# Stage ends and feed-forward openings of a two-block transformer kernel: another order of row-vector product, inverse and weight differences

## The chip, the cores and the metric

One core of one Trainium2 chip runs one program. The metric is the device time of a whole launch in microseconds. The median of 3 runs of the kernel before is 2208.19 us, lowest 2207.74, highest 2209.24.

## The reference

256 tokens of 1,024 values pass two blocks in fp32. The first block joins a recurrent branch and 16-head attention, followed by a retrieval layer of 16,384 experts. The second block has four feed-forward stages with a convolution stage and an attention stage between them. Each stage end and each feed-forward stage is this (cut):

```python
def rms_norm(x, g):
    x32 = x.astype(jnp.float32)
    y = x32 * lax.rsqrt(jnp.mean(x32 * x32, axis=-1, keepdims=True) + RMS_EPS)
    return (y * g.astype(jnp.float32)).astype(x.dtype)

def swiglu_ffn(h, w_gate_up, w_down):
    gate, up = jnp.split(h @ w_gate_up, 2, axis=-1)
    return (jax.nn.silu(gate) * up) @ w_down
...
        f = swiglu_ffn(rms_norm(x, ffn_norm_pre[layer, 0]), ffn_w_gate_up[layer, 0], ffn_w_down[layer, 0])
        x = x + MACARON_WEIGHT * rms_norm(f, ffn_norm_post[layer, 0])
```

The convolution and the attention stage end with `x = x + rms_norm(y, mix_norm_post[layer])` in the same way.

## The kernel before

**Weights.** All weights come as one stream of 664 chunks of 128 x 1024 fp32 (512 KB), in the order in which they are used, through a ring of RING = 3 buffers `raw`. ACT copies a chunk to fp32r (`whi`, L442, or L447 inside loops) and DVE subtracts to get what the copy lost (`wlo`, L915, or L920 inside loops). This is `split(c)` on both engines: ACT's part waits until the chunk has landed and until chunk c - 3 has been used by PE (`used`), DVE's part waits for ACT's. PE multiplies three times for each tile: high by high, high by low, low by high (L1586 to L1588 where the activations move, L1965 to L1967 where rows of tokens come out). SP loads chunk c + 3 when `wlo` of chunk c is made.

**Stage ends.** `bound(B)`, B = 0 to 7, stands in the program of each engine. B = 0 and 1 end the two halves of the first block; B = 2, 4, 5 and 7 end the feed-forward stages ffn0 to ffn3; B = 3 ends the convolution stage (`cout`), B = 6 the attention stage (`qo`). The stage's result lies in PSUM as four pieces of 128 tokens x 512 values (`wide`, r = 2t + half). ACT squares each piece and sums it (L482), and takes a root for each t (L487); DVE prepares one operand of the root (`half_of`, L960), inverts (`invert`, L965), and makes the new rows piece by piece in the order (t, half) = (0,0), (1,0), (0,1), (1,1): for B from 2 on `scaled` (L975) multiplies a piece by the inverse and by the norm vector (`rows_of`), and `added` (L981) adds it to the residual `htok` (tile res). Meanwhile PE runs 60 small bf16 matmuls without use (L1649). When the first two pieces are new, PE transposes them (`turn_half(B, 0)`, L1658), ACT scales and rounds the transposed tiles to `XH` (L497), DVE makes their rest `XL` (`lo_of_turned`, L945), and PE begins the next stage with its first two chunks (`first_pair`): the high products of tiles 0 to 3 (L1613, L1614), then `turn_half(B, 1)`, then the low products of tiles 0 to 3 (L1621), then high and low of tiles 4 to 7. `first_pair` waits at its head for `wlo` of both chunks.

**Feed-forward.** With b the stage's first chunk, chunks b and b + 1 are gate and up of the first 128 hidden values, then come gate, up, down in turn for the next ones: b + 2 gate, b + 3 up, b + 4 down of the first, b + 5 gate, b + 6 up and so on. The factor of the norm ahead of a stage is found while the first products run: ACT takes its root (`in_root`, L512), DVE inverts it (`in_inverse`, L1011), PE spreads it over the partitions (`in_spread`, L1640), and DVE copies it to `rstd` (`in_rstd`, L1015). DVE multiplies the gate by it (`gate_scaled`, L1430), ACT applies SiLU (L785), DVE forms the hidden values (`h_full`, L1436 and L1439), ACT rounds them (`h_hi`, L791) and DVE takes the rest (L1441), on which the down chunk waits. ACT has to load a table before its first SiLU (`preload`, L471). The order of the work on each engine is that in which the code issues it, and an engine that waits holds everything behind it.

## Time and profile before

| | |
|---|---|
| median of 3 runs | 2208.19 us |
| the profiled execution | 2207.9 us |
| its span on the core | 2205.9 us |
| PE busy | 2129.3 us, 97% |
| DVE busy | 1534.0 us, 70% |
| ACT busy | 1176.9 us, 53% |
| mean granted clock of PE | 0.991 |

The profiled execution is 0.3 us under the median, and 2.0 us of it lie outside the span. PE's busy time is made of modelled ends, each matmul's overlapping the next, so short pauses hardly show in it: they are read from the distance between starts. The lengths below are read in the same way, from one start to the next, wherever an order of work is followed.

### The profile page before, as it was taken

The numbers are of one execution on the slowest core, as the hardware profiler recorded it, in microseconds if no ns is written. First come the engines' busy times: TensorE is split into PE (matmuls) and PEld (weight loads), VectorE is DVE, ScalarE is ACT, GpSimd is POOL, SyncE is SP. The second block draws the span as 40 slices with busy tenths as digits, with TensorE's granted clock in tenths as the row PEclk, the third lists the DMA queues.
The fourth block names the chain that finished last, engine by engine and source line by source line (L and its number), as shares of the span: only waits on it lengthen the run. The fifth ranks groups of instructions, "written<-read, shape, count | busy, mean of one in ns | idle before, by whom it ended". The sixth has DMA issues, their size and how long they took to land.

```text
span 2205.9 us, 42158 instructions
## 1 busy us (share of the span) xinstructions
PE 2129.3 (97%) x15056; PEld 1953.2 (89%) x15056; DVE 1534.0 (70%) x2584; ACT 1176.9 (53%) x1996; POOL 52.8 (2%) x77
## 2 busy tenths in 40 slices
PE   7989999999999999999999999989999999999998
PEld 7888889999999988888888999878999999988997
DVE  7577665999899985555556666866666666676665
ACT  4755445656567664455455445445445444655444
POOL 0020000000100000000003000000000000000000
PEclk9999999999999999999999999999999999999999
DMA  5442354545443345555555665314554555444554
GB/s 204 153 146 94 106 174 152 186 170 183 159 138 119 131 155 196 192 191 194 195 191 193 231 218 192 134 46 165 184 186 154 183 186 184 168 146 137 185 185 142
DMA packets 101117, 366.47 MB, mean 166 GB/s; under 512 B 11504, under 2 KB 12144, under 8 KB 100528
## 3 DMA queue, kind: packets, MB, share of 16 engines
q1 hardware_dynamic: 97776, 352.59, 46.8%
q0 software_dynamic: 3264, 12.85, 1.6%
q8 instruction: 49, 0.80, 0.1%
q14 instruction: 28, 0.23, 0.0%
HBM read 363.29 MB, written 2.10 MB: 166 GB/s over the span
## 4 chain that ended last, share of the span: by engine, by line
PE 78%; DVE 12%; issue 5%; ACT 4%; DVEq 1%; DMA 0%; ACTq 0%
PE acc L1586 14%; PE acc L1588 13%; PE acc L1587 13%; PE wide L1965 9%; PE wide L1966 9%; PE wide L1967 9%; DVE wlo L915 3%; DVE arena L1372 2%; DVE res L1358 2%; ACT whi L442 1%; PE acc L2037 1%; PE sums L1797 1%; PE wide L1705 1%; PE wide L1707 1%; PE wide L1706 1%
## 5 line engine op out<-in xcount | busy, mean ns | idle before, releaser
L1586 PE MATMUL acc<-XH,whi 128*128 128x256 f32 (+1 forms) x3104 | 891.3, 287 | 9.9 <-DVE wlo L915 6.7
L1587 PE MATMUL acc<-XL,whi 128*128 128x256 f32 (+1 forms) x3104 | 878.6, 283 | 0.0
L1588 PE MATMUL acc<-XH,wlo 128*128 128x256 f32 (+1 forms) x3104 | 878.5, 283 | 0.0
L920 DVE TENSOR_TENSOR wlo<-raw,whi 128x1024 fp32r<-128x1024 f32 x396 | 484.6, 1225 | 304.5 <-ACT whi L447 284.5
L1586 PEld LDWEIGHTS acc<-XH,whi 128*128 128x128 f32 x3104 | 594.7, 192 | 23.7 <-DVE wlo L915 11.3
L1587 PEld LDWEIGHTS acc<-XL,whi 128*128 128x128 f32 x3104 | 595.0, 192 | 3.3
L1588 PEld LDWEIGHTS acc<-XH,wlo 128*128 128x128 f32 x3104 | 594.7, 192 | 0.0
L447 ACT ACTIVATE whi<-raw 128x1024 fp32r<-128x1024 f32 x456 | 479.8, 1053 | 182.8 <-PE wide L1967 181.7
L915 DVE TENSOR_TENSOR wlo<-raw,whi 128x1024 fp32r<-128x1024 f32 x268 | 328.3, 1227 | 142.1 <-ACT whi L442 131.4
L1965 PE MATMUL wide<-whi,small 128*128 128x512 f32 x896 | 351.7, 393 | 6.7 <-DVE wlo L915 3.8
L1966 PE MATMUL wide<-whi,small 128*128 128x512 f32 x896 | 350.6, 391 | 0.0
L1967 PE MATMUL wide<-wlo,small 128*128 128x512 f32 x896 | 349.6, 390 | 0.0
L442 ACT ACTIVATE whi<-raw 128x1024 fp32r<-128x1024 f32 x208 | 217.8, 1052 | 80.6 <-PE acc L1588 28.2
L1965 PEld LDWEIGHTS wide<-whi,small 128*128 128x128 f32 x896 | 169.2, 189 | 40.6 <-DVE wlo L915 4.6
L1967 PEld LDWEIGHTS wide<-wlo,small 128*128 128x128 f32 x896 | 168.8, 188 | 35.8
L1966 PEld LDWEIGHTS wide<-whi,small 128*128 128x128 f32 x896 | 169.1, 189 | 31.8
L785 ACT ACTIVATE arena<-arena 128x256 f32<-128x256 f32 x88 | 36.8, 418 | 192.5 <-DVE arena L1430 192.5
L791 ACT ACTIVATE small<-arena 128x256 fp32r<-128x256 f32 x88 | 36.7, 418 | 179.1 <-DVE arena L1439 179.1
L735 ACT ACTIVATE last_parts<-res,r2T 128x128 bf16<-128x128 bf16 x256 | 81.7, 390 | 58.3 <-DVE res L1358 58.3
L710 ACT ACTIVATE arena<-acc 128x256 f32 (+1 forms) x79 | 30.4, 385 | 94.8 <-PE acc L1588 94.6
L1441 DVE TENSOR_TENSOR small<-arena,small 128x256 fp32r<-128x256 f32 x88 | 37.4, 425 | 42.5 <-ACT small L791 42.5
L1430 DVE TENSOR_TENSOR arena<-acc,rstd 128x256 f32<-128x256 f32 x88 | 37.3, 424 | 39.3 <-PE acc L1588 38.9
(289 smaller groups left out, 2093.9 us busy)
## 6 DMA issues: line engine op xcount, KB each, us to landing
raw<-stream SPq DMA_DIRECT2D x664, 512.0 KB, 3.2
arena<-taps_in POOLq DMA_DIRECT2D x20, 256.0 KB, 4.0
arena<-rows_in POOLq DMA_DIRECT2D x7, 512.0 KB, 4.8
arena<-h_in SPq DMA_DIRECT2D x2, 544.0 KB, 4.2
res<-rgw SPq DMA_DIRECT2D x1, 1024.0 KB, 8.6
res<-tokens_in POOLq DMA_DIRECT2D x1, 1024.0 KB, 5.3
park<-res POOLq DMA_DIRECT2D x1, 1024.0 KB, 4.2
res<-park POOLq DMA_DIRECT2D x1, 1024.0 KB, 5.5
```

Source lines behind the costliest of these rows:

```text
L442: act.activation(whi[:, c % RING, :], raw[:, c % RING, :], ACT.Copy).then_inc(hi_done, 1)
L447: act.activation(whi[:, c % RING, :], raw[:, c % RING, :], ACT.Copy).then_inc(hi_done, 1)
L735: ins = act.activation(last_part(m % 2)[:, a, :], of_group(onehots, m % 2, 0)[:, a, 0, :], ACT.Copy, scale=r2T[:, bass.ds(4 * g + a, 1)])
L915: V.tensor_tensor(wlo[:, c % RING, :], raw[:, c % RING, :], whi[:, c % RING, :].bitcast(F32), ALU.subtract).then_inc(lo_done, 1)
L920: V.tensor_tensor(wlo[:, c % RING, :], raw[:, c % RING, :], whi[:, c % RING, :].bitcast(F32), ALU.subtract).then_inc(lo_done, 1)
L1358: V.tensor_tensor(pairs(onehots[:, s, 0, :]), of_tokens(e12, g), pairs(iotab[:, :]).to_broadcast([P, 8, NK // 2, 2]), ALU.is_equal)\
L1586: mm(out_, whi[:, s, w], xh, start=first, stop=False, **kw)
L1587: mm(out_, whi[:, s, w], xl, start=False, stop=False, **kw)
L1588: return mm(out_, wlo[:, s, w], xh, start=False, stop=last, **kw)
L1965: mm(dst, xh[:, x], whi[:, c % RING, w], start=first, stop=False, skip_group_check=True)
L1966: mm(dst, xl[:, x], whi[:, c % RING, w], start=False, stop=False, skip_group_check=True)
L1967: ins = mm(dst, xh[:, x], wlo[:, c % RING, w], start=False, stop=last, skip_group_check=True)
```

## The change

At stage ends from B = 2 on, the piece is multiplied by the norm vector first (`with_row`, into one of now four buffers `z`), which needs no inverse, and then one instruction multiplies by the inverse and adds the residual (`new_rows`). The weight difference (`wlo`) of the next stage's second chunk goes from before the stage end to behind the first two new pieces. In the stages that follow B = 1, 3, 4 and 6, the difference of chunk b + 2 goes between the two halves of `lo_of_turned`. 46 small matmuls instead of 60. In the opening of the feed-forward stages `in_spread` stands ahead of chunk b + 2, no longer in its middle; ACT splits b + 3 ahead of the table load, and b + 4 ahead of `h_hi`; DVE scales the first gate ahead of the difference of b + 3, and makes that of b + 4 ahead of the rest of the hidden values. The DVE wait on the norm vector's load comes first in the stage end.

```diff
-        z = ar(XN, 512, 2)
+        z = ar(XN, 512, 4)
...
-                in_root((1, 3, 4, 6)[f], ACT.Silu)
+                in_root((1, 3, 4, 6)[f], None)
                 split(b + 3)
+                preload(ACT.Silu)
                 silu(0, mb + 1)
+                split(b + 4)
                 h_hi(0, mb + 1, None)
...
-                    split_loop(c + 2, i, 6) if i is not None else split(c + 2)
+                    if k > 0:
+                        split_loop(c + 2, i, 6) if i is not None else split(c + 2)
...
+                def with_row(r):
+                    t, half = PIECES[r]
+                    dve.wait_ge(sem("out_sq"), 4 * B + r + 1)
+                    V.tensor_tensor(z[:, r, :], wide[:, r, :], rows_of[B - 1][:, half * 512:half * 512 + 512],
+                                    ALU.mult).then_inc(sem("with_row"), 1)
...
+                        dve.wait_ge(sem("with_row"), 4 * (B - 2) + NEW_ORDER.index((t, half)) + 1)
+                        ins = V.scalar_tensor_tensor(out=piece(htok, t, half), in0=z[:, r, :], scalar=inv,
+                                                     in1=piece(htok, t, half), op0=ALU.mult, op1=ALU.add)
...
                 else:
                     half_of(0)
-                if B > 0:
-                    dve.wait_ge(sem(f"row{B - 1}"), 16)
-                invert(0)
-                scaled(0, 0, 0)
-                half_of(1)
-                added(0, 0, 0)
-                invert(1)
-                for n in range(1, 4):
-                    scaled(*NEW_ORDER[n], n)
-                    added(*NEW_ORDER[n], n)
+                    with_row(0)
+                    invert(0)
+                    new_rows(0, 0)
+                    half_of(1)
+                    with_row(2)
+                    invert(1)
+                    new_rows(1, 0)
+                    split(BASE[ENDS[B]] + COUNT[ENDS[B]] + 1)
+                    with_row(1)
+                    new_rows(0, 1)
+                    with_row(3)
+                    new_rows(1, 1)
                 if NEXT[B] is not None:
-                    lo_of_turned(SPLIT[NEXT[B]], gain_of(NEXT[B]), turned_into)
+                    lo_of_turned(SPLIT[NEXT[B]], gain_of(NEXT[B]), turned_into, range(4))
+                    if B in (1, 3, 4, 6):
+                        split(BASE[ENDS[B]] + COUNT[ENDS[B]] + AHEAD)
+                    lo_of_turned(SPLIT[NEXT[B]], gain_of(NEXT[B]), turned_into, range(4, DT))
...
-                split(b + 2)
                 in_inverse((1, 3, 4, 6)[f])
-                split(b + 3)
                 in_rstd((1, 3, 4, 6)[f])
                 gate_scaled(0, b % RING, b + 1)
-                h_full(0, (b + 1) % RING, b + 2, mb + 1)
+                split(b + 3)
+                h_full(0, (b + 1) % RING, b + 2, mb + 1, b + 4)
...
-                split(b + 3 * MT - 1 + 2)
                 bound((2, 4, 5, 7)[f])
...
-                for _ in range((96, 84, 60, 60, 60, 60, 60)[B]):
+                for _ in range((96, 84, 46, 46, 46, 46, 46)[B]):
...
-                    gate(c, c + j, mb + k + 1 + jm if k else None,
-                         (lambda: in_spread((1, 3, 4, 6)[f])) if k == 0 else None)
+                    if k == 0:
+                        in_spread((1, 3, 4, 6)[f])
+                    gate(c, c + j, mb + k + 1 + jm if k else None)
```

The order of instructions shows the places. DVE at the end of ffn1 (B = 4), before: the first row is the difference of the next stage's second chunk, L960 is `half_of`, L965 `invert`, L975 `scaled`, L981 `added`.

```order
L915 TENSOR_TENSOR wlo<-raw,whi 128x1024
L960 TENSOR_SCALAR tiny<-tiny 128x1
L965 RECIPROCAL tiny<-tiny 128x1
L975 SCALAR_TENSOR_TENSOR arena<-wide,tiny,arena 128x512
L960 TENSOR_SCALAR tiny<-tiny 128x1
L981 TENSOR_TENSOR res<-res,arena 128x512
L965 RECIPROCAL tiny<-tiny 128x1
L975 SCALAR_TENSOR_TENSOR arena<-wide,tiny,arena 128x512
L981 TENSOR_TENSOR res<-res,arena 128x512
L975 SCALAR_TENSOR_TENSOR arena<-wide,tiny,arena 128x512
L981 TENSOR_TENSOR res<-res,arena 128x512
L975 SCALAR_TENSOR_TENSOR arena<-wide,tiny,arena 128x512
```

The same place of the change, where L973 is `with_row`, L985 `new_rows`, L963 `half_of`, L968 `invert` and L918 the weight difference:

```order
L963 TENSOR_SCALAR tiny<-tiny 128x1
L973 TENSOR_TENSOR arena<-wide,arena 128x512
L968 RECIPROCAL tiny<-tiny 128x1
L985 SCALAR_TENSOR_TENSOR res<-arena,tiny,res 128x512
L963 TENSOR_SCALAR tiny<-tiny 128x1
L973 TENSOR_TENSOR arena<-wide,arena 128x512
L968 RECIPROCAL tiny<-tiny 128x1
L985 SCALAR_TENSOR_TENSOR res<-arena,tiny,res 128x512
L918 TENSOR_TENSOR wlo<-raw,whi 128x1024
L973 TENSOR_TENSOR arena<-wide,arena 128x512
L985 SCALAR_TENSOR_TENSOR res<-arena,tiny,res 128x512
L973 TENSOR_TENSOR arena<-wide,arena 128x512
```

The weight difference went from the first row to the ninth, behind the second new piece, and one long instruction (L973) stands ahead of the first inverse.

ACT at the opening of ffn2, before, from `in_root` (L512) on: L442 are the copies of chunks b + 3, b + 4, b + 5, b + 6, L785 SiLU, L791 `h_hi`.

```order
L512 ACTIVATE tiny<-tiny 128x2
L471 ACT_TABLE_LOAD
L471 ACTIVATE tiny<-tiny 128x1
L442 ACTIVATE whi<-raw 128x1024
L785 ACTIVATE arena<-arena 128x256
L791 ACTIVATE small<-arena 128x256
L442 ACTIVATE whi<-raw 128x1024
L785 ACTIVATE arena<-arena 128x256
L442 ACTIVATE whi<-raw 128x1024
L791 ACTIVATE small<-arena 128x256
L442 ACTIVATE whi<-raw 128x1024
```

And in the change:

```order
L512 ACTIVATE tiny<-tiny 128x2
L442 ACTIVATE whi<-raw 128x1024
L471 ACT_TABLE_LOAD
L471 ACTIVATE tiny<-tiny 128x1
L785 ACTIVATE arena<-arena 128x256
L442 ACTIVATE whi<-raw 128x1024
L791 ACTIVATE small<-arena 128x256
L785 ACTIVATE arena<-arena 128x256
L442 ACTIVATE whi<-raw 128x1024
L791 ACTIVATE small<-arena 128x256
L442 ACTIVATE whi<-raw 128x1024
```

The copy of b + 3 went ahead of the table load, and that of b + 4 ahead of the first L791.

PE in the middle of chunk b + 2 of ffn2, before:

```order
L1586 MATMUL acc<-XH,whi 128x256
L1587 MATMUL acc<-XL,whi 128x256
L1588 MATMUL acc<-XH,wlo 128x256
L1640 MATMUL sums<-ident,tiny 128x128 x2
L1586 MATMUL acc<-XH,whi 128x256
```

And in the change, between `first_pair` and chunk b + 2 (its L1641 is L1621 of before, its L1606 to L1608 are L1586 to L1588, its L1660 is L1640):

```order
L1634 MATMUL acc<-XH,wlo 128x256
L1641 MATMUL acc<-XL,whi 128x256 x8
L1660 MATMUL sums<-ident,tiny 128x128 x2
L1606 MATMUL acc<-XH,whi 128x256
L1607 MATMUL acc<-XL,whi 128x256
```

The two `in_spread` halves (L1640 before, L1660 now) went from the middle of chunk b + 2 to its front.

## Rows read from the trace of the kernel before

**Rows 1.** The page, part 1: busy time of each engine, with its share.

```profile
PE 2129.3 (97%) x15056; PEld 1953.2 (89%) x15056; DVE 1534.0 (70%) x2584; ACT 1176.9 (53%) x1996; POOL 52.8 (2%) x77
```

**Rows 2.** The waits of PE: engine, tile, line, releaser; total us, times, longest.

```profile
PE wide L1965 <- DVE wlo L915: 3.8, 4, 1.1
```

**Rows 3.** Timeline of PE, end of ffn1 and opening of ffn2: start, us, line.

```profile
1690.97 3.52 PE L1649 MATMUL sums<-iotab 128*128 128x128 bf16 x60
...
1694.69 1.09 PE L1658 MATMUL wide<-ident,res 128*128 128x128 f32 x8 [0.20 <-DVE res L981]
...
1696.01 0.36 PE L1613 MATMUL acc<-XH,whi 128*128 128x256 f32 x1 [0.22 <-ACT XH L497]
...
1697.99 1.04 PE L1658 MATMUL wide<-ident,res 128*128 128x128 f32 x8
...
1698.79 1.19 PE L1621 MATMUL acc<-XL,whi 128*128 128x256 f32 x8
...
1699.81 0.28 PE L1613 MATMUL acc<-XH,whi 128*128 128x256 f32 x1
...
1701.73 1.12 PE L1621 MATMUL acc<-XL,whi 128*128 128x256 f32 x8
...
1702.80 0.39 PE L1586 MATMUL acc<-XH,whi 128*128 128x256 f32 x1
...
1704.33 0.60 PE L1640 MATMUL sums<-ident,tiny 128*128 128x128 f32 x4
...
1704.69 0.36 PE L1586 MATMUL acc<-XH,whi 128*128 128x256 f32 x1
...
1713.68 0.38 PE L1586 MATMUL acc<-XH,whi 128*128 128x256 f32 x1
...
1717.11 0.38 PE L1586 MATMUL acc<-XH,whi 128*128 128x256 f32 x1 [0.31 <-DVE wlo L915]
```

**Rows 4.** Timeline of PE, opening of ffn0.

```profile
1176.65 0.38 PE L1586 MATMUL acc<-XH,whi 128*128 128x256 f32 x1 [0.80 <-DVE wlo L915]
```

**Rows 5.** Timeline of DVE, the same stage end as Rows 3.

```profile
1689.60 1.23 DVE L915 TENSOR_TENSOR wlo<-raw,whi 128x1024 fp32r<-128x1024 f32 x1 [0.17 <-ACT whi L442]
...
1691.38 0.16 DVE L965 RECIPROCAL tiny<-tiny 128x1 f32<-128x1 f32 x1 [0.49 <-ACT tiny L487]
...
1691.58 0.75 DVE L975 SCALAR_TENSOR_TENSOR arena<-wide,tiny,arena 128x512 f32<-128x512 f32 x1
...
1693.16 0.75 DVE L975 SCALAR_TENSOR_TENSOR arena<-wide,tiny,arena 128x512 f32<-128x512 f32 x1
...
1693.95 0.69 DVE L981 TENSOR_TENSOR res<-res,arena 128x512 f32<-128x512 f32 x1
...
1696.72 0.69 DVE L981 TENSOR_TENSOR res<-res,arena 128x512 f32<-128x512 f32 x1
...
1697.33 1.65 DVE L945 SCALAR_TENSOR_TENSOR XL<-wide,vec,XH 128x256 fp32r<-128x256 f32 x4
```

**Rows 6.** Timeline of ACT, the same stage end and opening.

```profile
1690.52 0.20 ACT L482 ACTIVATION_READ_ACCUMULATOR arena<-wide 128x1 f32 x1
...
1690.98 0.29 ACT L487 ACTIVATE tiny<-tiny 128x1 f32<-128x1 f32 x1 [0.26 <-DVE tiny L960]
...
1701.96 1.28 ACT L471 ACT_TABLE_LOAD   x1
...
1703.36 1.04 ACT L442 ACTIVATE whi<-raw 128x1024 fp32r<-128x1024 f32 x1
...
1706.49 0.42 ACT L785 ACTIVATE arena<-arena 128x256 f32<-128x256 f32 x1 [2.08 <-DVE arena L1430]
```

**Rows 7.** Windows: length, busy us and count by engine, PE clock, DMA share.

```profile
1465.00:1467.50 2.50, 0.64 (x3) 0.34 (x2) 1.76 (x5) 0.73 (x2) 0.00 (x0) 0.50 0.00 0
...
1720.00:1760.00 40.00, 40.00 (x282) 37.54 (x281) 25.94 (x35) 17.61 (x23) 0.00 (x0) 1.00 0.57 190
```

**Rows 8.** Timeline of PE, at the start of cout.

```profile
1470.81 0.63 PE L1705 MATMUL wide<-whi,XH 128*128 128x512 f32 x1
```

More of the change, by code:

```diff
@@ L940, in norm_x, with lo_of_turned @@
                                            in1=rstd[:, 0:q.n], op0=ALU.mult, op1=ALU.mult).then_inc(sem("x_full"), 1)
-            def lo_of_turned(I, gain, src):
-                for k in range(DT):
+            def lo_of_turned(I, gain, src, ks):
+                for k in ks:
                     dve.wait_ge(sem("in_hi"), DT * I + k // 2 * 2 + 2)
@@ L985, in bound @@
                     dve.wait_ge(sem("unparked"), 16)
+                if B > 0:
+                    dve.wait_ge(sem(f"row{B - 1}"), 16)
                 if B < 2:
@@ L1241, in attention2 @@
                 split(QO_AT["o", 6] + AHEAD)
-                split(QO_AT["o", 7] + AHEAD)
             x_lo("o1")
@@ L1439, in h_full @@
                     V.tensor_tensor(hfull[:, m % 2, :], sgate[:, m % 2, :], acc[u3][:, 0:SEQ], ALU.mult).then_inc(sem("h_full"), 1)
+                    if then_split is not None:
+                        split(then_split)
                     dve.wait_ge(sem("h_hi"), cnt)
@@ L1541, in _ @@
                 x_lo("conv", k)
-            only_split("cout")
+            for k in range(7):
+                split(BASE["cout"] + k + AHEAD)
             bound(3)
@@ L1989, in ffn, with gate @@
                 b, mb = BASE[f"ffn{f}"], MT * f
-                def gate(c, at, cnt, halfway=None):
+                def gate(c, at, cnt):
                     pe.wait_ge(lo_done, at + 1)
```

30 lines of the change are left out of this document (16 added, 14 removed).

## The prediction

> **What bounds the kernel now.** I read the page first: PE is busy 97% of the span, far ahead of DVE and ACT [rows 1]. In the body of a feed-forward stage its matmuls stand without a pause: 282 in 40 us at the full clock, so 60 of them, a period of three chunks, take 8.51 us, with the DMA engines 0.57 busy [rows 7]. There PE sets the pace, and nothing that the change does to DVE or ACT counts. What can be won lies where PE stands still or runs matmuls without use. So the second view is PE's waits: ahead of the first down chunk PE waits for `wlo`, 3.8 us in 4 waits, one for each feed-forward stage [rows 2]. The third is PE's timeline over a stage end and an opening, read by starts [rows 3]; I take B = 4 as the pattern. Useful work stops at 1690.97, the useless matmuls follow, the transposes begin at 1694.69, 0.05 us behind the second new piece (1693.95 + 0.69, [rows 5]), and the first useful product at 1696.01, 1.32 us behind the transposes. Then `first_pair` runs without a gap (16 matmuls from 1699.81 to 1701.73 give 0.12 us for each). Its last 8 end at 1702.69; chunk b + 2 starts at 1702.80.
>
> **The opening.** From b + 2 (1702.80) to b + 6 (1717.11) PE takes 14.31 us. The work is one period (8.51), 24 matmuls (2.88) and `in_spread` (1704.33 to 1704.69, 0.36): 11.75. With 0.11 ahead of b + 2 and a first matmul of b + 6 that is 0.10 longer than the usual 0.28, 2.77 us are lost [rows 3, 7]. Does the new order take all of it away? Step by step, with `first_pair` ending at 1702.8:
> - `wlo` of b + 2 is made between the halves of `lo_of_turned`, some 2.5 us ahead of its use: no wait.
> - `in_spread` at 1702.8 feeds `rstd` by about 1703.9 and the scaled gate by 1704.3. b + 3 starts at 1702.8 + 0.36 + 2.88 = 1706.05, and its difference is ready by 1705.5: no wait.
> - ACT copies b + 3 when chunk b is used, at about 1702.5. A copy takes 1.06 to the next start, the table load with its small instruction 1.40 (1701.96 to 1703.36 [rows 6]), so the first SiLU starts at 1704.96, against 1706.49 now: 1.53 earlier.
> - b + 4's copy follows SiLU, at 1705.3 to 1706.35, its difference (1.23 [rows 5]) ends at 1707.6. PE wants it at 1706.05 + 2.88 = 1708.93. The largest wait is gone.
> - b + 6: its difference hangs on the SiLU chain, which starts 1.53 earlier and no longer has b + 4's 1.15 in it behind the first hidden values. So it is ready about 2.7 earlier, and PE gets there 2.6 earlier. That is a tie; I leave 0.1 there.
>
> So 2.65 for each of ffn1 to ffn3, 7.95 together. In ffn0 PE is idle 0.80 ahead of b + 2 [rows 4] and up to 1.1 ahead of b + 4 [rows 2], while the pause of some 0.4 ahead of b + 3 is missing: 3.3 by the same count. I take 2.9, as differences there run beside POOL's conversions (the 0.4 is an estimate). Bounds: nothing at all at the low end for b + 6 (0.6 less for each stage), the full 2.77 and 3.3 at the high end.
>
> **The stage end.** [rows 5, 6] for B = 4. The weight difference starts at 1689.60 and keeps `half_of` back until it ends, so the root comes at 1690.98, although the second square ends at 1690.72. Without it the root starts at 1690.74, 0.24 earlier. From the inverse (1691.38) to the end of the second new piece (1694.64) it is 3.26 now. Then it is 0.20 to the first long instruction, 0.67 for it (0.75 less an overlap of 0.08 with the next), 0.11 for `half_of`, 0.61 for `with_row`, 0.20, and 0.75: 2.54. That is 0.72 less: one long instruction now stands in the time before the inverse, where DVE waits for ACT. No row shows a product of a PSUM piece with a row alone; between 0.69 (L981, two SBUF operands) and 0.75 (L975, with PSUM and a scalar) I take 0.69, since L981 has the same form of instruction. The second piece is thus new at 1693.68, 0.96 earlier. 46 useless matmuls at 3.52/60 end at 1693.7: they neither hold it back nor leave a gap.
>
> But the difference has only moved. It runs from 1693.6 to 1694.83, just ahead of the first product (1693.73 + 1.32 = 1695.05), which waits for it. Behind it are the other four long instructions: 1694.75 + 0.73 + 0.67 + 0.73 + 0.75 = 1697.63, against 1697.41 now (1696.72 + 0.69). PE has done its 16 high products by 1697.03 and stands still for 0.6; the second transposes start at 1697.68, against 1697.99. The four L945 then start at 1697.55 and end at 1699.20. PE needs the last of them five low products before the end of that group, so the next group starts at 1699.20 + 0.60 + some 0.1 for restarts: 1699.9, against 1699.81 [rows 3]. **All of the 0.96 is given back here**, and 0.1 more. At B = 3 ACT's squares end later behind the difference, which leaves 0.1 of the 0.24: I take -0.25. The difference of b + 2 between the halves of L945 costs nothing: the second half is then ready from 1700.7 on, and PE's low products start at 1701.8.
>
> B = 2 and B = 5 lead into other stages, where the next wait is for DVE and ACT behind the second `XH` half. That half follows the second transposes, 0.3 earlier: 0.3 each. At B = 7 nothing of this follows and no difference is moved, so one long instruction less is 0.72.
>
> **The sum.** 7.95 + 2.9 + 2 x 0.3 + 0.72 - 2 x 0.1 - 0.25 = 11.7. The profiled execution of 2207.9 becomes 2196.2, and as the median of before is 0.3 above it, I forecast 2196.5. If `with_row` takes 0.75, four of them cost 0.12 to 0.24 at each of five ends, 1 us. The upper side of gain: restarts that cost nothing, ffn0's whole 3.3, 1.4 in all.
>
> **Rivals.**
> 1. *The SiLU chain is late.* Chunk b + 3's copy now stands ahead of the table load, so the load no longer hides behind the wait for chunk b. If SiLU starts 1.26 us later than I worked out, the difference of b + 4 still makes it (1.3 ahead), but b + 6 waits 1.2 in each of four stages: 4.8 of the gain goes, 2201.3. The rows speak against it: from the table load to the next copy it is 1.40 [rows 6]. The Trainium skill, in "ScalarE: Activation LUTs", section "What ACT_TABLE_LOAD costs", gives some 1.28 us for the load and about 1.38 more for a drain, 2.66 together; by it the sum would be that of this rival. The trace agrees with the load's 1.28 and shows no such second part at this place. Chance 0.13, with everything else that leaves half of the openings' waits.
> 2. *The moved difference costs more than counted*, each of five ends 0.5 to 1 us worse than -0.1: 2199 to 2201.5. For it speaks that DVE has no slack from 1693.6 to 1699.2. Against it, every length is in rows. Chance 0.1.
> 3. *No change.* The openings' gain is taken back in the body, by loads or by DVE. Against: 0.57 DMA share and no gap in 40 us [rows 7]. 2207 to 2210, chance 0.05.
> 4. *Slower: PE's clock falls at the stage ends.* Fewer useless matmuls and a new standstill of 0.6 plus waits of 0.4 us come in the same few microseconds. In the convolution stage the clock stood at half, 0.50, after little PE work (0.64 of 2.5 us [rows 7]), and a 512-column matmul took 0.63 us there [rows 8]. A half-clock stretch of 6 us holds some 3 us of full-clock work and costs 3 us. It decides if all five ends fall: 15 us, 2211.5. Against it, more than half of each such time is still matmuls. The Trainium skill, in "TensorE: Matmul & The Clock Gate", Part 4, says that transposes do not count as PE's activity for the clock, which would make these places thinner than they look. The trace can't tell, since the clock is full at every stage end. Chance 0.04.
>
> **How the numbers follow.** The forecast has 0.68; its own range is 2194 to 2199. Rivals 1 and 2 reach 2201.5. The half-clock stretch in the convolution stage can also fall a little longer or shorter, by 1.5 us. The range of 2193.3 to 2202.0 leaves out rivals 3 and 4 and 0.08 of the rest. A difference of 0.2%, 4.4 us, is about what a measurement of this kernel can tell from no change: faster takes the forecast and nearly all of 1 and 2, 0.9; same 0.06; slower 0.04.
>
> **What would show it.** Right: PE's waits for `wlo` ahead of L1965 are gone; from the end of the matmuls without use to `first_pair` 0.9 us less; a new wait of about 0.6 ahead of the second transposes and one ahead of the low products; useful work ends the group where it did. The table load stands behind a copy and SiLU starts 2 us behind `in_root`'s end plus a copy. The last piece ends 0.7 nearer to PE's last matmul. Wrong: a clock under 1.00 behind a stage end, a wait of over 0.5 at b + 6, or PE waiting at the head of `first_pair` for the moved difference (0.2 is all it has).

## The result, and the profile after

The changed kernel takes **2196.41 us** (median of 8 runs, 2194.78 to 2203.75), the kernel before on the same chip 2208.72 us (8 runs, 2207.16 to 2216.86). The ratio is 0.9944, with an interval of 0.9928 to 0.996. The forecast was 2196.5, within 2193.3 to 2202.0. The profiled execution took 2194.83 us, at a mean granted clock of 0.993 against 0.991.

The total is right, but not every term of it. To see that, the span is cut at marks that both kernels have: the first of the matmuls without use at each stage end. All of PE's work lies between these marks, so a stretch is shorter by what was won in it. "End" is the end of the span.

| stretch on PE | before | after | won | the prediction's terms |
|---|---|---|---|---|
| start to B = 1 | 1162.94 | 1160.27 | 2.67 | none |
| B = 1 to 2 (ffn0) | 197.75 | 196.73 | 1.02 | 2.9 |
| B = 2 to 3 (end B = 2, convolution) | 134.18 | 133.79 | 0.39 | 0.3 |
| B = 3 to 4 (end B = 3, ffn1) | 196.10 | 193.55 | 2.55 | 2.65 - 0.25 = 2.40 |
| B = 4 to 5 (end B = 4, ffn2) | 196.09 | 193.41 | 2.68 | 2.65 - 0.1 = 2.55 |
| B = 5 to 6 (end B = 5, attention) | 113.94 | 113.53 | 0.41 | 0.3 |
| B = 6 to end (end B = 6, ffn3, B = 7) | 204.9 | 201.7 | 3.2 | 2.65 - 0.1 + 0.72 = 3.27 |
| B = 1 to end | 1042.96 | 1032.73 | 10.2 | 11.7 |

Five stretches agree within 0.15 us. ffn0 gave 1.9 too little. And 2.67 us lie ahead of B = 1, where no term stood; they hid that miss.

The line numbers of the changed kernel are a little higher: its L918 is L915 of before, L985 is the new `new_rows`, L973 `with_row`, L1606 is L1586, L1633 is L1613, L1641 is L1621, L1660 is L1640, L1669 is L1649, L1678 is L1658, L1985 is L1965.

The page, its head and the part that answers to [rows 1]:

```profile
span 2193.0 us, 42029 instructions
...
PE 2121.2 (97%) x14986; PEld 1947.8 (89%) x14986; DVE 1534.5 (70%) x2584; ACT 1176.5 (54%) x1996; POOL 52.6 (2%) x77
```

PE issues 70 instructions fewer, which are 5 x 14 matmuls without use. Nothing else has left PE: the rest is standstill and time at half clock that are gone.

The waits of PE, where [rows 2] had 3.8 us for `wlo` ahead of L1965. Its successor L1985 has no such row any more. The first row below is for `wlo` ahead of the products of the activations (L1606), over the whole program; two of its 12 waits are read in ffn0 below. The second row is new and stands for the second transposes, one wait at each of five stage ends:

```profile
PE acc L1606 <- DVE wlo L918: 6.5, 12, 0.9
...
PE wide L1678 <- DVE res L985: 2.2, 5, 0.5
```

PE's timeline over the end of ffn1 and the opening of ffn2, as in [rows 3]:

```profile
1684.34 2.74 PE L1669 MATMUL sums<-iotab 128*128 128x128 bf16 x46
1686.97 1.09 PE L1678 MATMUL wide<-ident,res 128*128 128x128 f32 x8
1688.29 0.36 PE L1633 MATMUL acc<-XH,whi 128*128 128x256 f32 x1 [0.22 <-ACT XH L497]
...
1690.88 1.09 PE L1678 MATMUL wide<-ident,res 128*128 128x128 f32 x8 [0.45 <-DVE res L985]
1691.73 1.58 PE L1641 MATMUL acc<-XL,whi 128*128 128x256 f32 x8
1693.15 0.28 PE L1633 MATMUL acc<-XH,whi 128*128 128x256 f32 x1
...
1696.03 0.60 PE L1660 MATMUL sums<-ident,tiny 128*128 128x128 f32 x4
1696.39 0.36 PE L1606 MATMUL acc<-XH,whi 128*128 128x256 f32 x1
...
1707.84 0.35 PE L1606 MATMUL acc<-XH,whi 128*128 128x256 f32 x1
```

Read from the mark (1684.34; 1690.97 before). The transposes start at +2.63 instead of +3.72, so 1.09 are won. The second transposes start at +6.54 instead of +7.02, now behind a wait. The low products take 1.42 to the next group instead of 1.02, since they wait for DVE. `first_pair` ends at +11.69, where `in_spread` starts; before it ended at +11.72. The stage end gives nothing, as forecast. Behind it `in_spread` takes 0.36, and from chunk b + 2 to b + 6 it is 11.45 (1696.39 to 1707.84): with 0.36 that is 11.81, against 14.31 before. No wait stands in between.

DVE in the same stage end, as in [rows 5]:

```profile
1683.68 0.68 DVE L973 TENSOR_TENSOR arena<-wide,arena 128x512 f32<-128x512 f32 x1
...
1686.16 0.75 DVE L985 SCALAR_TENSOR_TENSOR res<-arena,tiny,res 128x512 f32<-128x512 f32 x1
1686.83 1.22 DVE L918 TENSOR_TENSOR wlo<-raw,whi 128x1024 fp32r<-128x1024 f32 x1
...
1690.08 0.75 DVE L985 SCALAR_TENSOR_TENSOR res<-arena,tiny,res 128x512 f32<-128x512 f32 x1
1690.74 1.65 DVE L948 SCALAR_TENSOR_TENSOR XL<-wide,vec,XH 128x256 fp32r<-128x256 f32 x4
```

`with_row` takes 0.68 (forecast 0.69). The second new piece is done at 1686.91, +2.57. The moved difference follows at once and ends at 1688.05, 0.24 ahead of the first product. The last new piece then ends at 1690.83, and PE's second transposes start 0.05 behind it. DVE works on that line without a pause.

ACT in the opening, as in [rows 6]:

```profile
1684.12 0.29 ACT L487 ACTIVATE tiny<-tiny 128x1 f32<-128x1 f32 x1
...
1695.81 1.06 ACT L442 ACTIVATE whi<-raw 128x1024 fp32r<-128x1024 f32 x1 [0.31 <-PE acc L1641]
1696.88 1.28 ACT L471 ACT_TABLE_LOAD   x1
...
1698.29 0.40 ACT L785 ACTIVATE arena<-arena 128x256 f32<-128x256 f32 x1
```

The root starts at -0.22 from the mark instead of +0.01: 0.23 earlier (forecast 0.24). The first SiLU starts at +13.95 instead of +15.52, 1.57 earlier (forecast 1.53).

**Ahead of B = 1.** The stretch from the mark of B = 0 (306.83 before, 306.60 after) to that of B = 1 holds 2.44 of the 2.67. Here are windows at the start of the stage that begins at 812; the columns are as in [rows 7], and the granted clock is the third number from the end. The kernel before:

```profile
810.00:815.00 5.00, 2.84 (x7) 2.29 (x8) 3.17 (x6) 3.46 (x6) 0.63 (x2) 0.56 0.93 355
815.00:820.00 5.00, 5.00 (x19) 3.94 (x18) 1.26 (x2) 1.36 (x2) 0.00 (x0) 0.75 0.42 170
```

The changed kernel:

```profile
810.00:815.00 5.00, 3.01 (x13) 2.54 (x14) 2.99 (x6) 3.46 (x6) 0.43 (x1) 1.00 0.96 370
815.00:820.00 5.00, 5.00 (x23) 4.14 (x23) 2.72 (x4) 2.73 (x4) 0.00 (x0) 1.00 0.67 254
```

Before, the granted clock fell to half there; after, it did not, though PE was busy for about 3 of the 5 us in both. The change touches nothing in this stretch. From B = 0 to B = 1 it was 856.1 in the kernel before and 856.3 in the experiment e3, which has the same fall; 854.4 in e9 and e11, where the clock fell there for a shorter time; 853.7 in the changed kernel and in the runs without a fall there; and 852.7 in e8, where another such stretch, near 590, is shorter. Here is e11, which is the changed kernel once more:

```profile
812.50:815.00 2.50, 2.50 (x7) 1.98 (x6) 0.28 (x1) 0.51 (x2) 0.00 (x0) 0.50 1.00 406
```

The same program fell in one run and not in the other, so I count these 2.4 us as chance, not as the change's.

**ffn0**, where the term failed. PE's waits in its opening, where [rows 4] had one of 0.80:

```profile
1177.37 0.39 PE L1606 MATMUL acc<-XH,whi 128*128 128x256 f32 x1 [0.89 <-DVE wlo L918]
...
1187.05 0.38 PE L1606 MATMUL acc<-XH,whi 128*128 128x256 f32 x1 [0.31 <-DVE wlo L918]
```

DVE there:

```profile
1169.82 1.66 DVE L948 SCALAR_TENSOR_TENSOR XL<-wide,vec,XH 128x256 fp32r<-128x256 f32 x4
...
1174.45 2.86 DVE L918 TENSOR_TENSOR wlo<-raw,whi 128x1024 fp32r<-128x1024 f32 x1
1177.24 1.25 DVE L1454 TENSOR_TENSOR arena<-arena,rstd 128x256 f32<-128x256 f32 x1
```

And POOL, which prepares the three bf16 parts of the convolution's bias:

```profile
1174.09 2.14 POOL L2148 TENSOR_TENSOR arena<-arena 32x1024 f32<-32x1024 f32 x1
1176.30 1.91 POOL L2149 CAST arena<-arena 32x1024 bf16<-32x1024 f32 x1
```

The difference of chunk b + 3 takes 2.86 instead of 1.22, and the 256-column product 1.25 instead of 0.42: 2.47 together, while POOL is at work. The new order has put them beside POOL's last two instructions. In the kernel before, the first difference met POOL's third instruction, and PE waited for that:

```profile
1174.44 1.06 POOL L2125 CAST arena<-arena 32x1024 bf16<-32x1024 f32 x1
...
1174.52 2.07 DVE L915 TENSOR_TENSOR wlo<-raw,whi 128x1024 fp32r<-128x1024 f32 x1
```

Which instructions meet is not fixed by the order alone. POOL's block starts when the load of the bias has landed: 7.43 us behind the mark in this run, 6.62 in e11. In e11, the same program, it met the difference of b + 2 instead, and ffn0 took 196.00, so there the gain was 1.75 and not 1.02:

```profile
1168.39 3.07 DVE L918 TENSOR_TENSOR wlo<-raw,whi 128x1024 fp32r<-128x1024 f32 x1
```

### The profile page after: what moved, and what is told of

Read it like the earlier page. It is cut to its first block, busy times and chain, and to the rows that moved or that the text cites. A ratio compares the mean times of both kernels' runs of the same rounds, so it can differ in the third digit from the quotient of the medians.

```text
span 2193.0 us, 42029 instructions
## 1 busy us (share of the span) xinstructions
PE 2121.2 (97%) x14986; PEld 1947.8 (89%) x14986; DVE 1534.5 (70%) x2584; ACT 1176.5 (54%) x1996; POOL 52.6 (2%) x77
## 4 chain that ended last, share of the span: by engine, by line
PE 80%; DVE 11%; issue 5%; ACT 3%; DVEq 1%; DMA 0%; ACTq 0%
PE acc L1606 14%; PE acc L1608 14%; PE acc L1607 14%; PE wide L1985 9%; PE wide L1986 9%; PE wide L1987 9%; DVE wlo L918 2%; DVE arena L1390 2%; DVE res L1376 2%; PE acc L2058 1%; PE sums L1817 1%; PE wide L1725 1%; PE wide L1726 1%; PE wide L1727 1%; DVE arena L1398 1%
## 5 line engine op out<-in xcount | busy, mean ns | idle before, releaser
L1606 PE MATMUL acc<-XH,whi 128*128 128x256 f32 (+1 forms) x3104 | 890.2, 287 | 7.7 <-DVE wlo L918 5.5
L1608 PE MATMUL acc<-XH,wlo 128*128 128x256 f32 (+1 forms) x3104 | 878.5, 283 | 0.0
L1606 PEld LDWEIGHTS acc<-XH,whi 128*128 128x128 f32 x3104 | 594.8, 192 | 18.6 <-DVE wlo L918 8.9
L1608 PEld LDWEIGHTS acc<-XH,wlo 128*128 128x128 f32 x3104 | 594.7, 192 | 0.0
L918 DVE TENSOR_TENSOR wlo<-raw,whi 128x1024 fp32r<-128x1024 f32 x268 | 329.4, 1231 | 130.8 <-ACT whi L442 120.0
L1985 PE MATMUL wide<-whi,small 128*128 128x512 f32 x896 | 350.3, 391 | 3.0 <-DVE small L1424 2.9
L442 ACT ACTIVATE whi<-raw 128x1024 fp32r<-128x1024 f32 x208 | 217.8, 1052 | 82.2 <-PE acc L1608 28.3
L1985 PEld LDWEIGHTS wide<-whi,small 128*128 128x128 f32 x896 | 168.6, 188 | 35.8 <-issue 3.3
L785 ACT ACTIVATE arena<-arena 128x256 f32<-128x256 f32 x88 | 36.7, 417 | 184.0 <-DVE arena L1448 184.0
L791 ACT ACTIVATE small<-arena 128x256 fp32r<-128x256 f32 x88 | 36.8, 418 | 177.4 <-DVE arena L1457 177.2
```

Source lines behind the costliest of these rows:

```text
L442: act.activation(whi[:, c % RING, :], raw[:, c % RING, :], ACT.Copy).then_inc(hi_done, 1)
L918: V.tensor_tensor(wlo[:, c % RING, :], raw[:, c % RING, :], whi[:, c % RING, :].bitcast(F32), ALU.subtract).then_inc(lo_done, 1)
L1606: mm(out_, whi[:, s, w], xh, start=first, stop=False, **kw)
L1608: return mm(out_, wlo[:, s, w], xh, start=False, stop=last, **kw)
L1985: mm(dst, xh[:, x], whi[:, c % RING, w], start=first, stop=False, skip_group_check=True)
```

## The experiments

Three batches were run, each with the kernel before on the same chip: medians 2209.92 (17 runs; e1 to e4), 2210.13 (14; e5 to e8) and 2209.16 (12; e9 to e11). Whole times of one kernel scatter by 4 to 12 us, so the stretches decide wherever less than some 3 us is in question. They are, in us (for e7, without such matmuls, from the end of the stage's useful work):

| | B=1 to 2 | to 3 | to 4 | to 5 | to 6 | to end |
|---|---|---|---|---|---|---|
| before | 197.75 | 134.18 | 196.10 | 196.09 | 113.94 | 204.9 |
| after | 196.73 | 133.79 | 193.55 | 193.41 | 113.53 | 201.7 |
| e1 openings only | 196.70 | 134.21 | 193.45 | 193.45 | 115.44 | 202.3 |
| e2 ends only | 198.09 | 134.12 | 195.81 | 195.68 | 113.54 | 204.0 |
| e3 difference ahead | 196.31 | 134.01 | 192.65 | 192.67 | 113.18 | 201.0 |
| e4 POOL later | 196.54 | 133.80 | 193.53 | 193.40 | 113.53 | 201.7 |
| e5 POOL spread | 196.08 | 135.38 | 193.55 | 193.41 | 115.02 | 201.8 |
| e6 60 useless | 196.31 | 135.66 | 193.54 | 193.40 | 115.07 | 201.8 |
| e7 0 useless | 197.02 | 135.93 | 193.67 | 193.87 | 113.54 | 202.2 |
| e8 table first | 196.06 | 135.38 | 193.87 | 193.72 | 115.08 | 202.1 |
| e9 no bias work | 194.47 | 133.77 | 193.54 | 193.41 | 113.54 | 201.7 |
| e10 combined | 194.46 | 135.02 | 192.66 | 192.66 | 113.18 | 201.1 |
| e11 change again | 196.00 | 134.50 | 193.53 | 193.40 | 114.95 | 201.7 |

The columns of ffn1 (B = 3 to 4) and ffn2 (B = 4 to 5) repeat to 0.02 where the kernels have the same order there. The convolution's and the attention's don't: half-clock stretches in them come and go (below). Nor does ffn0's, in which POOL's block lies differently from run to run.

### e1: the openings alone

Against the changed kernel: the stage ends, the moved differences and the 60 matmuls are as before.

```diff
-                    with_row(2)
-                    invert(1)
-                    new_rows(1, 0)
-                    split(BASE[ENDS[B]] + COUNT[ENDS[B]] + 1)
...
+                invert(1)
+                for n in range(1, 4):
+                    scaled(*NEW_ORDER[n], n)
+                    added(*NEW_ORDER[n], n)
...
+                split(b + 3 * MT - 1 + 2)
...
-                for _ in range((96, 84, 46, 46, 46, 46, 46)[B]):
+                for _ in range((96, 84, 60, 60, 60, 60, 60)[B]):
```

> The changed openings of the feed-forward stages, with the stage ends, the place of the second chunk's weight difference and the 60 useless matmuls of before. My theory: the gain is made in the openings. Measured on PE from the first useless matmul of a stage end to that of the next, ffn1 and ffn2 shorten by about 2.6 us each and ffn0 by about 1, as in the changed kernel; the two other stages by 0 and the end of the program by 0. In all 8.5 to 9.5 us, some 2199 to 2200. Rival (the earlier second piece at the stage ends carries the gain, with the openings' waits only moved): under 5 us of gain, over 2203, and ffn1 shorter by under 1.5.

Measured: 2201.38 us (6 runs, 2196.22 to 2204.66), ratio 0.9957 (0.994 to 0.9973). ffn1 and ffn2 are 2.65 and 2.64 shorter than before, exactly the term of 2.65. ffn0 gains 1.05, as in the changed kernel. So the openings' order, by itself, makes nearly the whole gain, and the shortfall in ffn0 belongs to it.

### e2: the stage ends alone

Against the kernel before: the new stage ends, the moved differences and 46 matmuls; the openings stay as they were.

```diff
-            only_split("cout")
+            for k in range(7):
+                split(BASE["cout"] + k + AHEAD)
...
-                for _ in range((96, 84, 60, 60, 60, 60, 60)[B]):
+                for _ in range((96, 84, 46, 46, 46, 46, 46)[B]):
```

> The changed stage ends alone (product with the norm vector ahead of the inverse, one weight difference behind the second new piece, 46 useless matmuls), with the openings of before. My theory: what is won up to the first transposes is given back before the second ones, so ffn1 and ffn2 are within 0.3 us of before, cin to cout and k2 to qo 0.4 shorter each, the program's end 0.7: 1.5 us in all, no measurable change (2207). Rival (0.96 us kept at each of five ends): 5 us and more faster, under 2203.5.

Measured: 2206.47 us (12 runs, 2203.6 to 2212.56), ratio 0.9984 (0.9972 to 0.9996). PE at B = 4 (mark 1688.56):

```profile
1691.20 1.09 PE L1670 MATMUL wide<-ident,res 128*128 128x128 f32 x8
...
1695.11 1.09 PE L1670 MATMUL wide<-ident,res 128*128 128x128 f32 x8 [0.46 <-DVE res L982]
...
1707.78 0.50 PE L1977 MATMUL wide<-whi,small 128*128 128x512 f32 x1 [0.89 <-DVE wlo L915]
```

The transposes come at +2.64 and +6.55 as in the changed kernel, and the openings' wait of 0.89 stays. ffn1 and ffn2 are 0.29 and 0.41 shorter (I had expected at most 0.3), because the SiLU chain, which is the bound in the old opening, starts a little earlier: at +15.11 at B = 4 instead of +15.52. In the new opening nothing is left of that: e1 and the changed kernel differ by -0.10 and +0.04 there. The two parts don't add up.

### e3: the difference back ahead of the stage end

```diff
-                    split(BASE[ENDS[B]] + COUNT[ENDS[B]] + 1)
...
+                split(QO_AT["o", 7] + AHEAD)
...
+                split(b + 3 * MT - 1 + 2)
...
-            for k in range(7):
-                split(BASE["cout"] + k + AHEAD)
+            only_split("cout")
```

> The changed kernel, with the weight difference of the second chunk back ahead of the stage end. My theory: DVE between the second piece and the low products is what gives the 0.96 us back, and the moved difference is 1.15 of that. With it ahead again the root comes 0.24 later, but there is no wait of 0.6 ahead of the second transposes, and each of five stage ends keeps some 0.7: 3 to 3.5 us faster than the changed kernel, about 2193; first_pair from the first useless matmul to its end 11.0 us at the end of ffn1, rather than 11.7. Rival (the moved difference is a gain, since half_of comes earlier): 1 us slower than the changed kernel, 2197.5.

Measured: 2196.68 us (6 runs, 2194.31 to 2200.67), ratio 0.9944 (0.993 to 0.9959). PE at B = 4 (mark 1686.46):

```profile
1689.41 1.09 PE L1678 MATMUL wide<-ident,res 128*128 128x128 f32 x8 [0.21 <-DVE res L985]
...
1692.71 1.04 PE L1678 MATMUL wide<-ident,res 128*128 128x128 f32 x8
...
1697.41 0.60 PE L1660 MATMUL sums<-ident,tiny 128*128 128x128 f32 x4
```

The first transposes come at +2.95, 0.32 later than in the changed kernel, the second at +6.25, 0.29 earlier and without a wait, and `first_pair` ends at +10.95 instead of +11.69. ffn1 and ffn2 are 0.90 and 0.74 shorter than after the change. Moving the difference is what gave the gain of the stage end back. My expectation of 3 to 3.5 us and a whole time of about 2193 was not met: the last four stretches are 2.7 us shorter together, and in whole times nothing shows. e4's median on the same chip is the same, with the half-clock stretch ahead of B = 1 in e3's profiled execution (856.3) on top.

### e4 and e5: POOL's bias work elsewhere

e4 moves the six instructions as a block behind the loads of taps and rows, into ffn0's body:

```diff
+            for n in range(20):
+                pool.wait_ge(used, BASE["ffn0"] + 4 + 2 * n)
...
             in_turn(pool.tensor_copy(bias_parts[0:96, :], bias[0:96, :]))
...
-            for n in range(20):
-                pool.wait_ge(used, BASE["ffn0"] + 4 + 2 * n)
```

> The changed kernel, with POOL's three conversions and two subtractions of the convolution's bias moved from the opening of ffn0 to behind its loads, in the body of ffn0. My theory: ffn0's opening gained 1.0 us in place of 2.9 because the weight difference of b + 3 took 2.86 us beside POOL's work. Without it, that difference takes 1.23, no wait of 0.89 at b + 3 and none of 0.31 at b + 6, and ffn0 shortens by 1.6 to 2.3 more: from 196.7 to about 194.8 between the useless matmuls; 2194.5 in all. Rival (ffn0's order itself is late, since the end of the first block has its own order): ffn0 stays at 196.7 and the wait at b + 3 stays. A third outcome is a loss in the body, where POOL now meets DVE: ffn0 not shorter although the wait at b + 3 is gone.

e5 issues them one by one, each behind every third of these loads:

```diff
+                if n == 2:
+                    in_turn(pool.tensor_copy(bias_parts[0:96, :], bias[0:96, :]))
+                if n == 5:
+                    in_turn(pool.tensor_tensor(bias_rest[0:96, :], bias[0:96, :], bias_parts[0:96, :], ALU.subtract))
...
+                prepare(n)
```

> The changed kernel, with POOL's six instructions on the convolution's bias set singly into the body of ffn0, one behind every third load of the taps, some 17 us apart. With the block of six moved as one, the opening of ffn0 lost nothing, but PE waited 1.81 us in the body for a weight difference that met the block. My theory: DVE and POOL hold each other up over pairs of their instructions, 1 to 2 us each time, and the body's slack takes one such delay but not six in a row. Then ffn0 shortens from 196.7 to about 194.6, with no wait of PE for a weight difference over 0.3 in it, and the kernel by 2 us against the change. Rival (any meeting costs PE its length): some six waits of 0.3 to 1 us in the body, ffn0 at 196 or more.

Measured: e4 2196.72 us (6 runs, 2194.74 to 2199.4), ratio 0.9945 (0.9932 to 0.9958); e5 2198.53 (6 runs, 2192.61 to 2202.88), ratio 0.9942 (0.9925 to 0.9959). In both the waits in ffn0's opening are gone, and yet ffn0 takes 196.54 and 196.08, no less than the changed kernel in its two runs (196.73 and 196.00). One wait stands in the body instead. e4, PE and then DVE:

```profile
1339.97 0.39 PE L1606 MATMUL acc<-XH,whi 128*128 128x256 f32 x1 [1.81 <-DVE wlo L923]
```

```profile
1335.54 2.40 DVE L1461 TENSOR_TENSOR small<-arena,small 128x256 fp32r<-128x256 f32 x1 [0.48 <-ACT small L791]
1337.86 3.19 DVE L923 TENSOR_TENSOR wlo<-raw,whi 128x1024 fp32r<-128x1024 f32 x2
```

POOL's block ran from 1328.20 to 1338.83 there. An instruction that takes 0.42 elsewhere took 2.40 beside it. e5, PE, DVE and POOL:

```profile
1217.52 0.39 PE L1606 MATMUL acc<-XH,whi 128*128 128x256 f32 x1 [1.36 <-DVE wlo L923]
```

```profile
1213.78 4.82 DVE L923 TENSOR_TENSOR wlo<-raw,whi 128x1024 fp32r<-128x1024 f32 x2 [0.53 <-ACT whi L447]
```

```profile
1214.21 2.15 POOL L2149 TENSOR_TENSOR arena<-arena 96x1024 f32<-96x1024 f32 x1
```

Two differences take 2.56 undisturbed (as in e4 at 1326.58) and 4.82 beside one POOL subtraction of 2.15: the 2.26 more are about that instruction's length. They fall on the first of the two, which takes 3.68 and ends 1.09 behind POOL's. This is the only place in which PE loses time against e9 (below), so POOL's other five instructions cost PE nothing. So moving POOL's work only moves the cost, unless each piece is shorter than the slack that DVE has. My expectation that ffn0 would be cured by e4 or e5 was wrong.

### e6 and e7: 60 and no useless matmuls

```diff
-                for _ in range((96, 84, 46, 46, 46, 46, 46)[B]):
+                for _ in range((96, 84, 60, 60, 60, 60, 60)[B]):
```

> The changed kernel with 60 useless matmuls at the stage ends again. My theory: DVE's line of four long instructions and four small ones decides when first_pair goes on, so the first transposes may start 0.75 us later at no cost: at the end of ffn1 they start at 3.4 in place of 2.6, the wait ahead of the second transposes goes to zero, and ffn1 and ffn2 stay within 0.15 us of 193.5. Rival (the fewer matmuls are a gain of their own): ffn1 and ffn2 0.6 to 0.8 us longer.

e7 is the same line with 0 in the five places.

> The changed kernel with no useless matmul at the ends B = 2 to 6. It asks whether they hold the clock. Rival 4 of the prediction: PE's clock falls to half behind the stage ends, a 128x256 product goes from 0.12 to 0.24 us there, and each end costs 1 to 3 us: 5 to 15 us slower than the change. If idle time of 2.6 us and the waits behind it do not reach that, the distances stay within 0.2 us of the change. I give the fall 0.6: before the convolution's end PE did as little, and the clock stood at half.

Measured: e6 2199.17 us (5 runs, 2196.46 to 2202.92), ratio 0.9954 (0.9937 to 0.997). PE's second transposes at B = 4 (mark 1685.92):

```profile
1692.52 1.04 PE L1678 MATMUL wide<-ident,res 128*128 128x128 f32 x8
```

The first transposes come 0.73 later (+3.36), the second at +6.60 with hardly a pause ahead, and ffn1 and ffn2 are the same to 0.01. The 14 matmuls fewer are worth nothing while the difference stands behind the first new pieces: DVE's line sets the end.

e7: 2199.8 us (5 runs, 2198.82 to 2204.62), ratio 0.9953 (0.9937 to 0.9969). PE at B = 4, and the window at the same place:

```profile
1695.85 1.09 PE L1678 MATMUL wide<-ident,res 128*128 128x128 f32 x8 [2.47 <-DVE res L985]
...
1697.55 0.41 PE L1633 MATMUL acc<-XH,whi 128*128 128x256 f32 x1
```

```profile
1696.00:1700.00 4.00, 3.78 (x22) 3.57 (x22) 3.93 (x6) 2.79 (x8) 0.00 (x0) 0.67 0.42 130
```

The granted clock fell to half (0.67 over these 4 us, 0.90 over the next 4), and a 256-column product started every 0.21 instead of 0.12. That happened at four of the five ends, B = 2, 3, 4 and 6. At B = 5 it did not. It cost little, 0.12 at B = 3 and 0.46 at B = 4. At B = 4 PE's 16 high products took 3.38 instead of 1.99. Of these 1.39 us, 0.60 fall into the standstill that the changed kernel has ahead of the second transposes, and 0.39 into its longer low products (1.03 against 1.42), which here no longer wait for DVE. The slower rival's mechanism is thus real, has its place where no matmul covers the wait, and is far smaller than 3 us an end.

### e8: table load first

```diff
-                in_root((1, 3, 4, 6)[f], None)
+                in_root((1, 3, 4, 6)[f], ACT.Silu)
...
-                preload(ACT.Silu)
```

> The changed kernel with ACT's table load ahead of the copy of b + 3 again. My theory: ACT is free at in_root's end, 0.25 us before chunk b is used; load and copy in either order end within 0.3 us of each other, so SiLU starts as before the swap or up to 0.25 earlier, and the copy of b + 3 is 1.15 later, its difference ending just about when PE wants it: ffn1 and ffn2 within 0.2 us of 193.5. Rival (the copy ahead of the load is what took the pause ahead of b + 3 away): a wait of 0.3 to 0.6 us ahead of b + 3 in each feed-forward stage.

Measured: 2199.1 us (5 runs, 2196.25 to 2203.35), ratio 0.995 (0.9933 to 0.9967). ACT at B = 4 (mark 1687.49):

```profile
1698.66 1.28 ACT L471 ACT_TABLE_LOAD   x1
...
1700.07 1.04 ACT L442 ACTIVATE whi<-raw 128x1024 fp32r<-128x1024 f32 x1
1701.02 0.40 ACT L785 ACTIVATE arena<-arena 128x256 f32<-128x256 f32 x1
```

I had expected ffn1 and ffn2 to stay within 0.2 us. SiLU itself starts 0.42 earlier (+13.53 against +13.95), but the copy of b + 3 starts 1.11 later (+12.58 against +11.47), and with it the difference that DVE makes of it. From there DVE's line is late up to b + 6, whose difference ends at 1711.21; PE starts on it at 1711.26, after a pause of 0.24 that the changed kernel does not have. ffn1 and ffn2 are 0.32 and 0.31 longer. So the copy's place ahead of the load is right and worth 0.3 a stage, and the tie at b + 6 is as narrow as the prediction had it.

### e9: no bias work

This kernel leaves the bias of the convolution's output out: POOL's six instructions are replaced by one small memset, so that only their time is missing.

```diff
-            in_turn(pool.tensor_copy(bias_parts[0:96, :], bias[0:96, :]))
-            in_turn(pool.tensor_tensor(bias_rest[0:96, :], bias[0:96, :], bias_parts[0:96, :], ALU.subtract))
...
+            pool.memset(bias_rest[0:1, 0:1], 0.0).then_inc(sem("bias_parts"), 1)
```

> The changed kernel without POOL's six instructions on the convolution's bias: the bias of the convolution's output is left out of the result. It asks what those six cost at all. My theory: they account for all that ffn0 lost against ffn1 apart from the other length of its first end (84 useless matmuls from 4.74 us on, in place of 2.6 to 2.8, so in_spread stands at 12.74 rather than 11.7 to 11.8). Then ffn0 is 193.5 + 0.95 = 194.5 us between the useless matmuls, with no wait in its opening and none in its body. Rival: ffn0 stays at 196, since something else in it (the taps' loads) holds DVE or the stream.

Measured: 2193.39 us (4 runs, 2192.52 to 2200.43), ratio 0.9934 (0.9911 to 0.9957). DVE in ffn0's opening:

```profile
1174.42 1.22 DVE L918 TENSOR_TENSOR wlo<-raw,whi 128x1024 fp32r<-128x1024 f32 x1
1175.67 0.43 DVE L1454 TENSOR_TENSOR arena<-arena,rstd 128x256 f32<-128x256 f32 x1
```

ffn0 takes 194.47 and has no wait in its opening. Against 197.75 before that is 3.28, the 3.3 of the prediction's count before POOL was taken off. So POOL's work, and nothing else, keeps 2.26 of it in the changed kernel (196.73), or 1.5 to 2.2 in the other kernels that have the new openings and POOL's block in its old place (1.53 in e11, the same program).

### e10: both lessons together, and e11: the change again

e10 has e3's edit, and POOL's bias work in halves of 512 columns, one behind each of twelve loads:

```diff
+                w = slice((n % 2) * 512, (n % 2) * 512 + 512)
+                job = n // 2 - 1
+                if job == 0:
+                    in_turn(pool.tensor_copy(bias_parts[0:96, w], bias[0:96, w]))
...
+                prepare(n)
```

> The changed kernel, with the second chunk's weight difference back ahead of the stage end (as in e3) and POOL's bias work in halves of 512 columns, one for each load of the taps in the body of ffn0. Theory: ffn1 and ffn2 at 192.7 as in e3, and ffn0 at about 194.0 to 194.5, since a delay of one DVE instruction by some 0.6 to 1.1 us fits into the body's slack. Against the change 3.3 us from the stage ends and 2.2 to 2.7 from ffn0: 5.5 us less in the profile's distances. If single meetings still cost PE a wait each, ffn0 stays at 196 and 3.3 remain.

> The changed kernel once more, on the same chip as the two others, since the whole time of a run also moves by some us with stretches at half clock that none of these edits makes. Expected: distances as before (ffn0 196.7, ffn1 193.55, ffn2 193.4), and a median of 2196 to 2199. The rival reading of the first result (that its 12.3 us are all the change's) asks for the part up to the first feed-forward stage to be shorter again by 2.4 us than in before; mine says that this part is 853.7 or 856.1 by chance.

Measured: e10 2197.19 us (6 runs, 2191.02 to 2198.24), ratio 0.9931 (0.9912 to 0.9949). e11 2198.44 (8 runs, 2194.79 to 2204.16), ratio 0.9952 (0.9935 to 0.9969). In e10 ffn0 takes 194.46 without a wait in it, although POOL's work is all done, and ffn1 and ffn2 take 192.66. From B = 1 to the end that is 1029.0, against 1034.1 for e11 on the same chip and 1032.7 for the first run of the change. Of the kernels that do all the work it is the best by its stretches, by 0.8 us against e3; by whole times the intervals overlap, so on those alone its lead isn't certain. e11 repeats the change's stretches in ffn1 and ffn2 to 0.02, and gets 196.00 in ffn0. From B = 0 to B = 1 it takes 854.4, between the two values that I had named. At 812 it is 1.6 us slower than the first run, since the clock falls there again, and near 590 it is 0.8 faster, where a half-clock stretch is shorter. So the rival reading, that the change itself shortens this part, is refuted: the fall at 812 is back in the same program.

## Why the prediction was right, and where it was not

- **The openings, 2.65 each: right.** 2.65 and 2.64 in e1, no wait from b + 2 to b + 6, SiLU earlier by 1.57 against 1.53. The tie at b + 6 is there: its first matmul takes 0.35, not 0.28.
- **ffn0, 2.9: wrong.** It gave 1.02 in the first run and 1.75 in e11. The step that failed is "I take 2.9, as differences there run beside POOL's conversions (the 0.4 is an estimate)". The meetings cost DVE up to the whole length of the POOL instruction that runs beside it: in the first run POOL's last two held up a difference and a product by 2.47 together. Against e9 the price is 2.26 in the first run and 1.53 in e11, and not 0.4; the 3.3 without it was right (3.28). A row of before had it: the first difference there took 2.07 beside a POOL cast. I had taken its cost off as something past, and did not lay the new DVE order beside POOL's times.
- **The stage end, "all of the 0.96 is given back": right.** +11.69 against +11.72. The second new piece came at +2.57 (forecast +2.71), the second transposes waited 0.45 by the row, 0.6 by the starts. e6 and e3 show the reason from both sides: earlier transposes are worth nothing while DVE's line has the difference in it, and 0.74 to 0.90 when it is out.
- **B = 2 and B = 5, 0.3 each: right in size** (0.41 at B = 5, where `in_spread` starts at +13.12 instead of +13.36). At B = 2 PE is 0.42 earlier at +11.79, right behind `first_pair`; the 0.39 of the whole stretch alone would not show it, since the convolution's half-clock stretch varies by more.
- **B = 3, -0.25, and B = 4 and 6, -0.1: small and slightly too dark.** The end cost 0.10 at B = 3 and gained 0.04 at B = 4, against e1. The stretches don't part B = 6 from B = 7.
- **B = 7, 0.72: mis-sized.** From the last matmul's start to the end of DVE's last row it is 5.72 instead of 6.22, so 0.50. Ahead of the second new piece DVE stands still for 0.39, which at B = 4 it does not; it does so in every run with the new stage ends, and why, no run tells.
- **Rival 1 (SiLU late) refuted**: 1.41 from the table load's start to SiLU. The Trainium skill, in "ScalarE: Activation LUTs", section "What ACT_TABLE_LOAD costs", gives some 1.28 for the load, with which the row agrees, and about 1.38 for a drain, which does not show between the load and the ACTIVATE behind it.
- **Rivals 2 and 3 did not come**: the moved difference cost what was counted, within 0.15 in ffn1 and ffn2, and in the bodies of ffn1 to ffn3 PE has no new wait.
- **Rival 4 (clock) did not come**: the granted clock is 1.00 over both windows from the mark to b + 6. e7 shows that it would with no matmul in the wait, and costs 0.1 to 0.5.
- **The total** was hit in part by luck: two errors have opposite signs, 1.9 too much in ffn0, and 2.4 given by a half-clock stretch that the profiled execution of the kernel before had at 812 and the changed one had not. The profiled executions differ by 13.1 us, the medians by 12.3, where the sum says 11.7. Without chance the change is worth 10.2 us by the stretches of the first profile; the medians of the last batch differ by 10.7 (2209.16 less 2198.44), with an interval of some 7 to 14 from their ratio.

## What to carry to other kernels

Work that is moved off a waiting place stays in the same engine's line: lay that line out behind the new place before counting the gain, and look for the next wait on it. Lay the line also beside the other engines' times, POOL's above all, and cut POOL's pieces until each is shorter than DVE's slack. Where the clock falls in one run and not in the next, compare distances between marks that both kernels have, and only in stretches without such a fall; 0.3 us is sure there where whole times scatter by several. Run the same kernel twice before a stretch is trusted: ffn0 moved by 0.7 us with nothing changed.

## What the runs showed of the hardware

**POOL and DVE hold each other up.** Beside POOL instructions that read SBUF, DVE's instructions with two SBUF operands are stretched by up to the whole time of POOL's: 1.22 to 2.86 and 3.07, 0.42 to 1.25, 0.42 to 2.40, and two differences from 2.56 to 4.82 beside one of 2.15. POOL's are stretched too (a 32 x 1024 cast from 1.03 to 1.91). `lo_of_turned`, with one operand in PSUM, keeps its 1.65 beside POOL's subtraction (1169.82 in ffn0). The Trainium skill, in "SBUF — State Buffer", section "Who interferes with whom", says that a DVE instruction with two SBUF inputs and a GpSimd instruction that reads SBUF exclude each other for a whole instruction. The trace agrees: the difference of 1174.45 would run from 1176.23, where POOL's row ends, to 1177.45 by it, and ended at 1177.31. Which of the two goes first is not always the one whose row starts first: in e5 the difference starts at 1213.78 and POOL's subtraction at 1214.21, and yet POOL's takes its usual 2.15, and the difference ends 1.09 behind it.

**Half-clock stretches come and go.** With nothing changed at the place, the clock fell at 812 in four of the 13 profiles: in the kernel before and in e3, and for a shorter time in e9 and e11. In the other nine it did not. In the attention stage it fell in e11 and not in the first run of the same kernel. e11:

```profile
1935.00:1940.00 5.00, 5.00 (x28) 4.74 (x28) 2.46 (x5) 1.10 (x4) 0.00 (x0) 0.70 0.34 105
```

The first run of the change:

```profile
1935.00:1940.00 5.00, 4.48 (x34) 4.18 (x34) 3.66 (x10) 2.15 (x5) 0.00 (x0) 1.00 0.41 143
```

It costs some 1.4 us there (114.95 against 113.53). At 812 PE's standstill was 2.89 to 2.90 us in all 13 profiles, so its length alone does not decide whether the clock falls; what does, no run tells. The largest part of the scatter of whole times lies ahead of B = 0, where nothing was changed either: that mark stands at 305.8 to 307.2 in eight profiles, at 309.4 in e8, and at 312.2 to 312.9 in e1, e5, e7 and e10. In these five the mean granted clock from 85 to 100 is 0.89, in the first run of the change it is 1.00. This is why e10, the best by its stretches, does not lead by its profiled execution.
